# An expert layer with a more even spread of its side work, and 43 gathered rows scaled by ACT and added by GpSimd

## What is computed

```python
def peer(h, w_query, query_gain, sub_keys_1, sub_keys_2, expert_down, expert_up):
    def block(hb):                                   # 128 tokens
        qry = rms_norm((hb @ w_query).reshape(128, 8, 256), query_gain)
        s1 = einsum("thd,nd->thn", qry[..., :128], sub_keys_1)
        s2 = einsum("thd,nd->thn", qry[..., 128:], sub_keys_2)
        v1, i1 = top_k(s1, 16); v2, i2 = top_k(s2, 16)
        ...                                          # top 16 of the 256 sums, per head
        u, vv = expert_down[experts], expert_up[experts]   # (128, 8, 16, 1024) each
        act = gelu(einsum("thkd,td->thk", u, hb))
        return einsum("thk,thkd->td", gates * act, vv)
```

## Time and profile before

| | us |
|---|---|
| runs, median of 3 | 3631.07 (3629.5 to 3632.62) |
| profiled execution, its own time | 3627.36 |
| its span | 3625.5 |
| first gather issued | 2097.9 |
| dot of row 256 (chunk 2) starts | 2968.8 |
| busy over the span: PE / DVE / ACT / POOL | 3074.4 / 2134.3 / 1181.6 / 600.2 |

### The profile page before, as it was taken

One profiled execution on the slowest core, in us unless ns is written; L12 is line 12 of the kernel. 1 busy time (PEld: TensorE's weight loads), 2 busy tenths in 40 slices (PEclk: granted clock), 3 DMA queues, 4 the chain that ended last, 5 costly groups with the idle time before them and its releaser, 6 DMA issues.

```text
span 3625.5 us, 34677 instructions
## 1 busy us (share of the span) xinstructions
PE 3074.4 (85%) x12138; PEld 2109.4 (58%) x12138; DVE 2134.3 (59%) x4304; ACT 1181.6 (33%) x2353; POOL 600.2 (17%) x540
## 2 busy tenths in 40 slices
PE   5989999798777989998998877987997677777777
PEld 4868888587555768886777743654564222222222
DVE  6655443776455454432452689776647988855555
ACT  2233222443444442222652345632222121211111
POOL 0000000000000000000000022233334454444442
PEclk9999999899888999998999998999999889999999
DMA  5534444243111324442312375977999999999997
GB/s 219 188 123 140 140 146 139 76 140 99 36 41 47 119 91 145 140 142 80 112 50 70 105 302 196 345 289 302 372 372 380 406 392 421 422 422 421 421 422 331
DMA packets 147547, 797.82 MB, mean 220 GB/s; under 512 B 16304, under 2 KB 18480, under 8 KB 81712
## 3 DMA queue, kind: packets, MB, share of 16 engines
q0 software_dynamic: 73728, 536.90, 36.9%
q1 hardware_dynamic: 69840, 251.69, 20.6%
q10 hardware_dynamic: 3808, 7.02, 0.5%
HBM read 793.46 MB, written 2.10 MB: 219 GB/s over the span
## 4 chain that ended last, share of the span: by engine, by line
PE 61%; DVE 15%; DMA 14%; ACT 5%; issue 4%; POOL 0%; DVEq 0%; SPq 0%; ACTq 0%; POOLq 0%
PE psum L153 61%; DMA tail<-in_experts,tail 14%; DVE tail L187 4%; ACT arena L164 2%; DVE tail L170 2%; DVE arena L182 2%; ACT L164 1%; DVE tail L193 1%; DVE tail L190 1%; DVE region L170 1%; PE psum L158 1%; DVE tail L182 1%; DVE tail L196 1%; ACT region L164 1%; DVE tail L205 1%
## 5 line engine op out<-in xcount | busy, mean ns | idle before, releaser
L153 PE MATMUL psum<-tail,arena 128*128 128x256 f32 (+2 forms) x3652 | 1319.9, 510 | 306.6 <-ACT arena L164 282.2
L153 PE MATMUL psum<-rounded,rounded 128*128 128x512 f32 x5496 | 1293.1, 396 | 40.8 <-DVE rounded L182 28.2
L153 PEld LDWEIGHTS psum<-tail,arena 128*128 128x128 f32 x3652 | 690.3, 200 | 895.5 <-issue 835.4
L153 PEld LDWEIGHTS psum<-rounded,rounded 128*128 128x128 f32 x5496 | 1036.1, 190 | 280.7 <-issue 56.1
L216 POOL DMA_INDIRECT tail<-in_experts,tail x512 | 580.1, 1133 | 1862.4 <-DVE tail L199 949.5
L187 DVE CUSTOM_DVE_ANT_0 tail<-tail 128x1024 f32<-128x1024 f32 x512 | 625.9, 1223 | 332.0 <-DMA tail<-in_experts,tail 329.9
L170 DVE TENSOR_TENSOR rounded<-arena,rounded 128x1024 fp32r<-128x1024 f32 (+2 forms) x285 | 316.5, 1111 | 346.7 <-ACT rounded L164 346.5
L164 ACT ACTIVATE rounded<-arena 128x1024 fp32r<-128x1024 f32 (+2 forms) x317 | 291.9, 939 | 446.2 <-DVE arena L170 238.9
L164 ACT ACTIVATE tail<-tail 128x1 f32<-128x1 f32 (+3 forms) x544 | 115.4, 213 | 978.2 <-DVE tail L187 812.6
L153 PE MATMUL psum<-arena 128*128 128x1 f32 (+3 forms) x792 | 198.8, 376 | 78.0 <-ACT arena L164 48.1
L164 ACT ACTIVATE arena<-psum 128x256 f32<-128x256 f32 (+2 forms) x210 | 97.7, 481 | 461.3 <-PE psum L153 461.1
(11 more groups left out here) (82 smaller groups left out, 1532.7 us busy)
## 6 DMA issues: line engine op xcount, KB each, us to landing
arena<-in_ada SPq DMA_DIRECT2D x136, 512.0 KB
arena<-in_fin SPq DMA_DIRECT2D x88, 512.0 KB
arena<-in_win SPq DMA_DIRECT2D x56, 512.0 KB
arena<-in_fout SPq DMA_DIRECT2D x32, 512.0 KB
arena<-in_mxbc SPq DMA_DIRECT2D x32, 512.0 KB
arena<-in_pq SPq DMA_DIRECT2D x32, 512.0 KB
arena<-in_ain SPq DMA_DIRECT2D x24, 512.0 KB
arena<-in_mz SPq DMA_DIRECT2D x16, 512.0 KB
```

The costliest lines, as they stand in the source:

```text
L153: return self.e.matmul(o, a, b, start=start, stop=stop, skip_group_check=skip)
```

## The change

It has two parts. **The spread**: in chunks 0 and 1 every call takes one main step; in chunk 0 two rank steps follow it, in chunk 1 none; once the main steps are used up a call takes two rank steps. Main steps now come ahead of the rank steps of a call. The first 14 rank steps of chunk 2 go into the main steps of the query projection (one each, from its seventh step). That makes 64 main steps in chunk 0 and 42 in chunk 1.

**A third adder**: rows with s = 7, 11, ... 119 in chunk 0 (29 rows) and s = 11, 19, ... 115 in chunk 1 (14 rows), 43 in all (the words that came with the change say 44), and all of them PE's before, are scaled in place by ACT (128x1024 instead of the 128x128 diagonal) and added by POOL to a sum of its own, `fin_pool`, 4 x 256 columns in memory that the diagonals and unused halves of buffers had; the first of a chunk is copied instead. POOL does the addition of row n - 6 ahead of the gather of row n. `dve_finish` adds `fin_pool` to `fin_out` in chunks 0 and 1, and the diagonals have 6 buffers instead of 8.

```diff
-        diag = [tmp[i][:, 128 * j:128 * j + 128] for i in (6, 7) for j in range(4)]
+        at_tmp = raw_at + 4096
+        fin_pool = tiles(arena[:, at_tmp + 1536:at_tmp + 3584], 4)[:, :, 256:512]
+        diag = [tmp[6][:, 0:128], tmp[6][:, 128:256]] + [tmp[7][:, 128 * j:128 * j + 128] for j in range(4)]
...
-            yield from par(act_pq(e, f), both(act_tok(e, 2 * f), act_tok(e, 1) if f == 0 else wait_steps(3)))
+            yield from par(act_pq(e, f), both(act_tok(e, 2 * f), act_tok(e, 1) if f == 0 else wait_steps(3)),
+                           both(wait_steps(6), first(ranks, 14)))
...
+        def adder(n):
+
+            c, s = n // 128, n % 128
+            if 4 <= s < 120 and (s % 4 == 3 if c == 0 else s % 8 == 3 if c == 1 else False):
+                return "pool"
+            return "dve" if s >= 24 and (s % 4 == 1 if c < 2 else s % 16 == 9) else "pe"
...
         def pool_gather(e):
             for n in range(512):
                 c, i = n // 128, n % 128
+                if n >= 6 and adder(n - 6) == "pool":
+                    pool_add(e, n - 6)
                 e.wait_ge(*idx_ok.at(c))
...
+        def pool_add(e, n):
+            c, i = n // 128, n % 128
+            v = tiles(SLOTS[slot_no[n]][:, 1024:2048], 4)
+            e.wait_ge(*g_scaled.at(n))
+            before = [m for m in rows_of("pool", c) if m < n]
+            if before:
+                e.wait_ge(*g_pool.at(before[-1]))
+                e.tt(fin_pool, fin_pool, v, ALU.add).then_inc(*g_pool.tick(n))
+            else:
+                if c:
+                    e.wait_ge(*pool_free.at(c - 1))
+                e.copy(fin_pool, v).then_inc(*g_pool.tick(n))
...
             for i in range(GG):
-                if own_add(n + i):
+                if adder(n + i) == "pool":
+                    v = SLOTS[slot_no[n + i]][:, 1024:2048]
+                    e.wait_ge(*g_in.at((c, grp)))
+                    e.act(v, v, ACT.Copy, scale=d[:, i:i + 1]).then_inc(*g_scaled.tick(n + i))
+                if adder(n + i) != "pe":
                     continue
...
         def dve_finish(e, c):
-            e.wait_ge(*g_mm.at(128 * c + 127))
-            e.wait_ge(*g_own.at(max(n for n in range(128 * c, 128 * c + 128) if own_add(n))))
+            e.wait_ge(*g_own.at(rows_of("dve", c)[-1]))
+            if c < 2:
+                e.wait_ge(*g_pool.at(rows_of("pool", c)[-1]))
+                e.tt(tiles(fin_out, 4), tiles(fin_out, 4), fin_pool, ALU.add).then_inc(*pool_free.tick(c))
+                e.wait_ge(*pool_free.at(c))
+            e.wait_ge(*g_mm.at(rows_of("pe", c)[-1]))
...
         def steps_of(c, grp, main, ranks):
 
-            if c == 0:
-                some(ranks, 2)
-                some(main, 2 if grp % 4 == 3 else 1)
-            elif c == 1 and next(main, True) is None:
-                pass
+            if c < 2 and next(main, True) is None:
+                some(ranks, 2 if c == 0 else 0)
             else:
-                some(ranks, 1)
+                some(ranks, 2 if c == 1 else 1)
```

More of the change, by code:

```diff
@@ L2103, in pe_main, with act_main @@
             yield from par(pe_pq(e, f), both(pe_tok(e, 2 * f), pe_tok(e, 1) if f == 0 else wait_steps(3)))
-        def act_main(e, f):
+        def act_main(e, f, ranks=iter(())):
             yield from act_norm(e, 4, f)
@@ L2158, in build @@
         g_in = landed("expert_landed", len(SLOTS))
[L2159 to L2166, removed]
+        g_own, g_scaled, g_pool, pool_free = [signal(n) for n in (
+            "expert_added_own", "expert_scaled", "expert_added_pool", "pool_sum_free")]
+        def adder(n):
[3 more added lines that the diff above has]
+            return "dve" if s >= 24 and (s % 4 == 1 if c < 2 else s % 16 == 9) else "pe"
+        rows_of = lambda who, c: [n for n in range(128 * c, 128 * c + 128) if adder(n) == who]
+        by_pe = [n for n in range(512) if adder(n) == "pe"]
         turn = {n: i for i, n in enumerate(by_pe)}
-        added = lambda n: g_own.at(n) if own_add(n) else g_mm.at(n)
+        added = lambda n: {"pe": g_mm, "dve": g_own, "pool": g_pool}[adder(n)].at(n)
         stored = landed("stored", 2)
@@ L2184, in dve_dots @@
             for m in range(n - 8 * GG, n - 7 * GG) if n >= 8 * GG else ():
-                e.wait_ge(*(g_own.at(m) if own_add(m) else g_diag.at(m)))
+                e.wait_ge(*(g_own.at(m) if adder(m) == "dve" else g_diag.at(m) if adder(m) == "pe" else g_scaled.at(m)))
             for i in range(GG):
@@ L2208, in act_diag @@
             for i in range(GG):
-                if own_add(n + i):
+                if adder(n + i) == "pool":
[3 more added lines that the diff above has]
+                if adder(n + i) != "pe":
                     continue
                 k = turn[n + i]
-                if k >= 8:
-                    e.wait_ge(*g_mm.at(by_pe[k - 8]))
-                e.act(diag[k % 8], ident, ACT.Copy, scale=d[:, i:i + 1]).then_inc(*g_diag.tick(n + i))
+                if k >= len(diag):
+                    e.wait_ge(*g_mm.at(by_pe[k - len(diag)]))
+                e.act(diag[k % len(diag)], ident, ACT.Copy, scale=d[:, i:i + 1]).then_inc(*g_diag.tick(n + i))
         def pe_add(e, c, grp):
@@ L2219, in pe_add @@
                 n = 128 * c + s_i
-                if own_add(n):
+                if adder(n) != "pe":
                     continue
@@ L2228, in pe_add @@
                 for u in range(2):
-                    ins = e.mm(ps["acc", c, u], diag[turn[n] % 8], SLOTS[slot_no[n]][:, 1024 + 512 * u:1536 + 512 * u],
-                               s_i == 0, s_i == 127)
+                    ins = e.mm(ps["acc", c, u], diag[turn[n] % len(diag)], SLOTS[slot_no[n]][:, 1024 + 512 * u:1536 + 512 * u],
+                               s_i == 0, n == rows_of("pe", c)[-1])
                 ins.then_inc(*g_mm.tick(n))
@@ L2249, in dve_add @@
                 n = 128 * c + GG * grp + i
-                if not own_add(n):
+                if adder(n) != "dve":
                     continue
@@ L2253, in dve_add @@
                 e.wait_ge(*g_act.at((c, grp)))
-                before = [m for m in range(128 * c, n) if own_add(m)]
+                before = [m for m in rows_of("dve", c) if m < n]
                 if before:
@@ L2324, in act_experts @@
         def act_experts(e):
-            main = act_main(e, 1)
+            ranked = [act_topk(e, c) for c in range(4)]
+            main = act_main(e, 1, ranked[2])
             before_rows(main, iter(()))
-            drive(act_topk(e, 0))
+            drive(ranked[0])
             for g, (c, grp) in enumerate(ALL_GROUPS):
                 if grp == 0:
-                    ranks = iter(()) if c == 3 else act_topk(e, c + 1)
+                    ranks = iter(()) if c == 3 else ranked[c + 1]
                     late = act_tok(e, 3) if c == 2 else iter(())
@@ L2342, in dve_experts @@
         def dve_experts(e, ranks):
-            main = dve_main(e, 1)
+            ranked = [ranks] + [dve_topk(e, c) for c in range(1, 4)]
+            main = dve_main(e, 1, ranked[2])
             before_rows(main, ranks)
@@ L2347, in dve_experts @@
                 if grp == 0:
-                    ranks = iter(()) if c == 3 else dve_topk(e, c + 1)
+                    ranks = iter(()) if c == 3 else ranked[c + 1]
                     late = wait_steps(3) if c == 2 else iter(())
```

## The result

| | before | changed |
|---|---|---|
| median of 7 runs, us | 3630.72 (3625.7 to 3637.73) | 3621.65 (3616.64 to 3628.6) |
| span of the profiled execution | 3625.5 | 3620.8 |

The ratio is 0.9973, with a 95% interval of 0.9963 to 0.9983: faster by 9.8 us, 6 to 13 (the two medians alone differ by 9.1). The forecast was 3619, 12 faster.

A forecast was written before the change was run, and what follows sets the result against it. Chunks 2 and 3 run at the gathers' pace; earlier stretches are bound by DVE, PE or DMA in turn. Stage gains and losses (1 + 25 + 7 + 6 + 2 + 10.5 - 17 - 24 + 1.5) sum to 12: 3631 - 12 = 3619 us, range 3587 to 3657.

The forecast's parts named there:

- the signs that it named: Rows 32 to 77: DMA near 0.9, PE below 0.85; rows 212 to 229: DVE near 0.95; POOL additions 2.3 to 3.6 us.
- the forecast's 155: Rows 32 to 77: PE 125, DVE 134, DMA 141 us, taken as 141 / 0.91 = 155 against 180 before; gain 25.
- 1.7 was set: Rows 0 to 31: DVE's price of a main step, 1.7 us; four steps fewer and 7 POOL rows gave 144 against 145.5.
- b: What DVE loses for each of the 43 POOL additions: taken as 0.8 us, between 0 and 2.4.
- this delay lies under transfers: POOL's addition ahead of gather n delays gathers, but a gather is under way for 10.4 us; taken at nothing, uncovered 2.4 us each.
- PE's relief: The third adder takes 43 x 2.0 = 86 us off PE, 58 of them in chunk 0.
- The price of 2.0 us a row: PE's time for one of its rows, 77.6 / 39 = 2.0 us.
- divided the largest load by 0.85: Rows 78 to 113, inversion: DVE 101.5, PE 86, DMA 101 us; over 0.85, 119 against 126, gain 7.
- The crowded ranks: Rows 212 to 229: 18 rank steps at two a call make DVE bound, 71 us against 47, loss 24.
- the full DMA in rows 172 to 211: Query projection: DMA 124, now near 128 us, 14 rank steps hidden; before 111, loss 17.
- rival 3: Rows 32 to 137: stages set by waits between engines, PE's relief buys nothing; sum +1, 3630 us; chance 0.20.
- Rival 1: Chunks 0 and 1: POOL's additions hold DVE for their whole length, b = 2.4; 3663 us; chance 0.26.

The follow-up runs named there:

- e1: Changed kernel with no POOL rows, the 43 rows staying with PE (the spread alone): 3613.5 us, ratio 0.9949 to the kernel before.
- e2: Changed kernel with the 43 POOL rows but the side steps placed as before (the third adder alone): 3633.2 us, ratio 1.000 to the kernel before.
- e3: Changed kernel, but each of POOL's 41 additions adds 4 of the 1024 columns: 3586.8 us, ratio 0.9868 to the kernel before.
- e9: Changed kernel with four-column POOL additions, each preceded by two zero fills that hold POOL about as long without reading: 3605.1 us, ratio 0.992.
- e5: Changed kernel, but POOL adds row n - 7 instead of n - 6 ahead of gather n: 3625.3 us, ratio 0.9974 to the kernel before.
- e8: Changed kernel with four-column POOL additions, and ACT scales only 4 columns of the 43 rows as well: 3587.7 us, ratio 0.9877.
- e7: Changed kernel with the last 18 rank steps one a call and only 9 POOL rows, in chunk 0's inversion: 3582.2 us, ratio 0.9856.
- e4: Changed kernel, but once chunk 1's main steps are used up a call takes one rank step, not two: 3606.5 us, ratio 0.9923.

## Why the prediction was right in its number, and where its steps were not

**The time and the sign held**: 3621.65 against 3619, in the range. The ledger went 864.5 to 855.2, and six of its nine lines lie within 4 us of the forecast. (For before, the prediction spread its stretches evenly over their rows: it has 180 and 126 us for rows 32 to 77 and 78 to 113, where the cut at the dots gives 185.1 and 119.7.) Most of the signs that it named came too: POOL's additions of 2.34 to 3.32 us, dots of chunk 0 with a mean of 1.27 us, DVE busy 0.97 of rows 212 to 229; in rows 32 to 77 DMA is at 0.85 (near 0.9 was said) and PE at 0.86 (below 0.85). But errors that cancel stand behind the sum, so that it is right to 3 us is luck in part, and a reader should take the parts by their own runs.

**The gain's owner was not asked for, and then guessed wrong.** The prediction priced both parts together and never one alone; what was expected of e1 and e2 gave the gain to the adder. The prediction's own unit prices would have shown it: with the 11 POOL rows of rows 32 to 77 back on PE, that stage is 125 + 22 = 147 us of PE, over 0.96 = 153, no longer than the forecast's 155 with them. e1 measured 148. The stage gains because five main steps left it, not because PE lost rows. Rows 0 to 31 were priced too low as well: four main steps fewer took 9.8 us off DVE in e1, 2.4 each where 1.7 was set, and the stretch became 13 us shorter. By the runs: spread alone -18.5, adder alone 0, both -9.8. On top of the spread the third adder loses 8 us.

**b, the term for DVE's wait, was too small.** It was set at 0.8 us a row; DVE's 53.6 us more, less 2.5 for the two additions in the finish, make 51 / 43 = 1.2. Against e3, where the additions are short, it is 54.2 us, 1.3 for each of the 41. On the path that costs 17 to 20 us (e9 to the change). The sentence "Dots and own additions have two SBUF inputs; rank steps, and main steps that read PSUM, mostly have one" held as far as it goes, but it isn't the whole list. Of DVE's 51 us the dots have 15.5, and the 62 own additions have nothing (mean 1286 ns, 1285 before), since none began beside an addition of POOL's. As much as the dots, 15.6, has the gate's product on one column, with two SBUF inputs, which the prediction left out. Some 16 have scalings of data in SBUF, main steps with one input. The changed kernel, POOL and DVE in time:

```profile
2309.88 2.35 POOL L170 TENSOR_TENSOR arena<-arena,tail 128x1024 f32<-128x1024 f32 x1 [6.53 <-ACT tail L164]
...
2397.78 2.49 POOL L170 TENSOR_TENSOR arena<-arena,tail 128x1024 f32<-128x1024 f32 x1 [7.24 <-ACT tail L164]
...
2462.28 2.43 POOL L170 TENSOR_TENSOR arena<-arena,tail 128x1024 f32<-128x1024 f32 x1 [1.69 <-ACT tail L164]
...
2475.11 2.36 POOL L170 TENSOR_TENSOR arena<-arena,tail 128x1024 f32<-128x1024 f32 x1 [2.97 <-ACT tail L164]
```
```profile
2311.31 1.07 DVE L176 TENSOR_SCALAR tail<-arena 128x256 f32<-128x256 f32 x1 [1.50 <-ACT arena L164]
...
2397.97 3.38 DVE L187 CUSTOM_DVE_ANT_0 tail<-tail 128x1024 f32<-128x1024 f32 x1
...
2462.42 2.30 DVE L170 TENSOR_TENSOR tail<-tail 128x1 f32<-128x1 f32 x1
...
2475.86 1.28 DVE L170 TENSOR_TENSOR tail<-tail,psum 128x512 f32<-128x512 f32 x2 [0.82 <-PE psum L153]
```

The product of one column, 0.16 us by itself, began 0.14 us after POOL's addition and ended with it. The dot at 2397.97 ended 1.1 us after POOL's addition did and took 3.38 instead of 1.22. The scaling of 256 columns took 1.07 instead of 0.35. The two products of 512 columns with one input in PSUM took 1.28 together, their usual time, in the middle of an addition. Nor was any instruction of a rank step that began beside an addition longer than usual. The Trainium skill, in "SBUF — State Buffer", section "Who interferes with whom", says that a DVE instruction with two SBUF inputs contends with a GpSimd instruction that reads SBUF, that one in a 2-port mode contends too, and that whoever comes second "fully blocks"; it lists `tensor_scalar` among those that can enter such a mode. This trace agrees in that both kinds were held to the end of the addition; in which mode the scalings ran it doesn't show. I had weighed the first half of the rule and not the second.

**POOL's own time was taken at nothing and wasn't.** The step "this delay lies under transfers" held for the early place (e5: nothing) but not for the length: e9, which holds POOL 2.25 us a row and hardly touches DVE, is 18 us slower than e3, 0.4 us a row. The likely reason, argued and not shown by a trace, is that the additions take their time in a queue in which the next gathers stand. Which stretch loses how much of it is read from single profiles and not settled.

**PE's relief was priced at 86 us and was some 50.** All of PE's rows in chunks 0 and 1 together kept it busy 421.0 us before and 370.4 after, 50.6 less for 43 rows less. A matrix instruction of 128x512 took 660 ns in the mean before and 719 after, and over these rows the granted clock was 0.91 before and 0.86 after. In rows 0 to 31 it is plainest: 673 ns at a granted clock of 0.85, 807 ns at 0.73, so that seven rows fewer saved half a microsecond of PE. The price of 2.0 us a row had been read where the clock was 0.98. It cost the sum little, since PE was the largest load in none of its stages up to row 137.

**PE's relief was worth nothing where PE was fullest and everything where it wasn't.** In rows 32 to 77 (PE 0.96 in e1, but DMA 0.93 too) the kernel with four-column additions, with 11 rows fewer on PE, took 153.8 us against 148.2. In e8's profile, where ACT's scaling is short as well, it is 148.6. That points to the scaling for the 5 us in this stretch, by single profiles, though e8 is not faster as a whole (rows 78 to 113 take 112.8 us there for 109.4 in e3). Even then 11 rows of relief bought nothing. In the inversion (PE 0.8) nine rows of relief gave 20.7 us for 19.0 us of PE. There PE and DVE answer each other level by level, and a row's matrix product in PE's queue delays the next level; DVE's waits for PE, 18.3 us shorter in e7, bear this out. The prediction divided the largest load by 0.85 there and so could not see this; its 119 us came close because spread (+13) and relief (-19) were both missed.

**The crowded ranks were right**: 71 forecast, 68.3 measured, loss 19 for 24; e4 gives 15 us back by spreading them over rows 212 to 247. So was the full DMA in rows 172 to 211 (128 forecast, 124.5), and rival 3's thought that stages are not set by loads holds for the inversion alone.

**The rivals.** Rival 1 named the right mechanism for about half of the adder's loss and overpriced it: POOL's additions hold DVE for 1.2 to 1.3 of their 2.47 us, not for all, and not all on the path. The prediction put the point from which it decides at b = 1.25. The measured b lies at that point, where the sum said no gain, and the kernel is 10 us faster: the spread gave more than was thought. Rival 2's DMA share of 0.94 to 0.96 in rows 32 to 137 came in none of the kernels with the spread (at most 0.93, 0.92 and 0.91 in the three stretches); its time of 3583 was reached in another way (e7).

## What to carry to other kernels

Price the parts of a change one by one even if they come together: the sum was right here by 3 us while the part that was thought to bring the gain lost 8. An engine's share of busy time doesn't tell by itself what relief is worth. Where PE and DVE answered each other, work taken out of PE's queue counted in full at a share of 0.8; where PE was at 0.96 and DMA at 0.93, it bought nothing. So offload where the waits of the other engine name the one that is relieved. In e7 nine rows instead of 43 are worth 17 us, where the 43 lose 8; with the spread (18.5) and the single rank steps (14.4) that makes the 50 us below the kernel before. A unit price of PE holds at the clock at which it was read. When side work is moved to be even, look at its end too: the last steps must not be crowded to finish early when nobody waits for them.

## What the runs showed of the hardware

- An addition of 128x1024 on POOL takes 2.35 us in the median (mean 2.47, longest 3.32), and a copy of 1024 columns 1.04, so the addition with its two inputs took 2.3 times the copy. The five longest, 3.2 to 3.3 us, all began while a dot was running: the hold goes both ways.
- While it runs, even a one-column DVE product with two SBUF inputs waits for its end (2.30 us instead of 0.16), and so do one-input scalings of SBUF data (1470 ns in the mean for 435 on 384 columns). Products with one input in PSUM and the instructions of rank steps that began beside an addition kept their usual length. POOL's fills, which read nothing, lengthened no dot (mean 1223 ns in e9, as in e3); DVE's busy time rose by 5.4 us there, nearly all of it on one-input scalings (2.7 on those of 384 columns, 1.1 on those of 256).
- PE's granted clock was 0.73 in rows 0 to 31 of the changed kernel against 0.85 before, with PE busy 0.69 of the time for 0.71; a matrix instruction of 128x512 took 807 ns for 673. It cost nothing that these runs show, since DVE was busy 0.94 of that stretch.
